# Moving the deviation and the normalisation of the gated values inside the feature stage of a one-core decoder step

## The reference, cut to what matters

```python
def gmlp_gate(u, v, ws, bs, ln_g, ln_b):
    u = jax.nn.gelu(u)
    vn = layer_norm(jax.nn.gelu(v).reshape(b, t, G_B, DG_B), ln_g, ln_b)
    ...
    mixed = jnp.einsum('gts,bnsgd->bntgd', w, vn.reshape(b, nc, c, G_B, DG_B))
    mixed = mixed + jnp.swapaxes(bs[:, :c], 0, 1)[:, :, None].astype(vn.dtype)
    return u * mixed.reshape(b, t, W_B), vn.reshape(b, t, W_B)
```

## Time and profile before

| | |
|---|---|
| median of 3 runs | 1611.86 us (1606.54 to 1611.88) |
| the profiled execution, its time | 1607.65 us |
| its span in the trace | 1605.9 us |
| TensorE busy | 1392.5 us, 87% of the span |
| VectorE, ScalarE, GpSimd busy | 644.2, 549.5, 158.1 us |
| mean granted TensorE clock | 0.928 of full speed |
| feature stage, TensorE's last product to next stage's first | 12.14 us without a matmul |

### The profile page before, as it was taken

How to read it: one execution, slowest core, us unless ns; L and a number is a source line. 1 busy time by engine, 2 the same in 40 slices (tenths; PEclk the granted TensorE clock), 3 DMA queues, 4 the chain that set the end, 5 groups by cost and what they waited for, 6 DMA issues and landing times. The chain is left out here.

```text
span 1605.9 us, 25617 instructions
## 1 busy us (share of the span) xinstructions
PE 1392.5 (87%) x9998; PEld 982.1 (61%) x9999; DVE 644.2 (40%) x1021; ACT 549.5 (34%) x1070; POOL 158.1 (10%) x152
## 2 busy tenths in 40 slices
PE   4998999689999989887997998989982799998980
PEld 2444999665568767776886996767862233333320
DVE  3331554248731223343875002337546223322226
ACT  1222324148740633444222213433120343332325
POOL 0000000003310023220000000000000122222210
PEclk9999999879997979999998999999995799999995
DMA  9111121114001340001304104635234488787336
GB/s 329 51 49 40 33 59 40 50 54 157 1 27 34 100 145 16 2 3 37 131 40 144 40 14 171 249 106 175 106 127 187 175 275 284 245 303 237 83 62 226
DMA packets 83684, 185.03 MB, mean 115 GB/s; under 512 B 12948, under 2 KB 48923, under 8 KB 77171
## 3 DMA queue, kind: packets, MB, share of 16 engines
q1 hardware_dynamic: 76523, 157.14, 27.6%
q0 software_dynamic: 6912, 25.17, 6.7%
q10 hardware_dynamic: 144, 1.25, 0.2%
HBM read 144.31 MB, written 39.31 MB: 114 GB/s over the span
## 5 line engine op out<-in xcount | busy, mean ns | idle before, releaser
L3068 PE MATMUL bank<-arena,hT 128*64 x384 | 178.0, 608 | 10.1 <-DVE hT L3184 5.7
L3068 PEld LDWEIGHTS bank<-arena,hT 128*64 128x64 f32 x384 | 51.4, 140 | 112.4 <-issue 109.6
L479 PE MATMUL bank<-arena,hT 128*128 128x512 f32 x256 | 112.1, 596 | 0.0
L2140 PE MATMUL bank<-hT_rest,f_w_high 128*128 128x352 f32 x288 | 93.9, 326 | 0.0
L3071 PE MATMUL bank<-arena,hT 128*64 128x512 f32 x192 | 91.0, 620 | 0.0
L3094 PE MATMUL bank<-arena,hT 128*64 x192 | 87.5, 598 | 0.7 <-ACT hT L3135 0.7
L3071 PE MATMUL bank<-h,hT 128*64 128x512 f32 x192 | 87.0, 596 | 0.0
L479 PEld LDWEIGHTS bank<-arena,hT 128*128 128x128 f32 x256 | 48.5, 192 | 57.9 <-issue 57.9
L3024 POOL DMA_INDIRECT expert_sums<-hT,row_slot x24 | 47.4, 1973 | 222.0 <-DVE hT L3190 142.4
L2139 PE MATMUL bank<-hT_high,q_w_high 128*128 128x352 f32 x192 | 62.5, 326 | 4.0 <-DVE q_w_low L2432 4.0
L2139 PE MATMUL bank<-f_h_high_a,f_w_high 128*128 128x352 f32 x180 | 59.2, 329 | 6.7 <-DVE f_w_low L689 6.7
(11 more groups left out here) (494 smaller groups left out, 3181.2 us busy)
## 6 DMA issues: line engine op xcount, KB each, us to landing
arena<-in_ex_wg_dram SPq DMA_DIRECT2D x16, 1024.0 KB, 4.9
arena<-in_ex_wu_dram SPq DMA_DIRECT2D x16, 1024.0 KB, 8.5
arena<-in_ex_wd_dram SPq DMA_DIRECT2D x16, 1024.0 KB, 12.3
tokens<-h SPq DMA_DIRECT2D x24, 512.0 KB, 2.6
arena<-in_cache_mem_k_dram SPq DMA_DIRECT2D x8, 1024.0 KB, 4.9
arena<-in_w_in_dram SPq DMA_DIRECT2D x12, 512.0 KB, 4.0
h<-tokens SPq DMA_DIRECT2D x6, 1024.0 KB, 7.2
h<-in_x_prompt_dram SPq DMA_DIRECT2D x8, 512.0 KB, 8.7
```

The lines of the kernel that those rows point to most:

```text
L479: last = nc.tensor.matmul(ps[bank][0:r, 0:n], hT[:, k, i * P:i * P + r], wt[:, k, col:col + n], start=(k == 0), stop=(k == KC - 1))
L2140: nc.tensor.matmul(out, high, w_low, start=False, stop=False)
L3068: nc.tensor.matmul(ps[UPB[u % 2]][rows_of(0), :], xT[:, u % 2, k, rows_of(0)], gate_up_of[:, bass.ds(slot, 1), :, k, :].rearrange("p a g f ...
```

## The change

ScalarE's table load, its wait for `stats` and its two instructions for the deviation stand in the loop over blocks behind block 2. On VectorE the wait for the deviation and the three passes stand between `low_w(10)` and `low_w(11)`.

```diff
                 if n == 2:
                     act.wait_ge(cw_mm, 1)
                     nc.scalar.copy(cw, ps[7][:, 0:168].rearrange("p (c n) -> p c n", c=6)).then_inc(cw_ok, 1)
+                if n == 2:
+                    nc.scalar.preload_act_table_set(EXPLN)
+                    act.wait_ge(stats, 1)
+                    link(nc.scalar.activation(mom[:, 1, :], mom[:, 1, :], ACT.Ln, bias=c.eps, scale=1.0 / DH))
+                    nc.scalar.activation(mom[:, 1, :], mom[:, 1, :], ACT.Exp, scale=-0.5).then_inc(rstd_ok, 1)
                 if n >= 4:
                     if n - 4 < 6:
                         conv_silu(n - 4)
-            nc.scalar.preload_act_table_set(EXPLN)
-            act.wait_ge(stats, 1)
-            link(nc.scalar.activation(mom[:, 1, :], mom[:, 1, :], ACT.Ln, bias=c.eps, scale=1.0 / DH))
-            nc.scalar.activation(mom[:, 1, :], mom[:, 1, :], ACT.Exp, scale=-0.5).then_inc(rstd_ok, 1)
...
-            for n in range(10, len(plan)):
-                low_w(n)
+            low_w(10)
             dve.wait_ge(rstd_ok, 1)
             link(nc.vector.tensor_tensor(vg, vg, bc(mom[:, 1, :]), ALU.mult))
             dve.wait_ge(ln_in, 32)
             link(nc.vector.tensor_tensor(c.vg, c.vg, c.A("glng").unsqueeze(1).to_broadcast([P, TILES, 256]), ALU.mult))
             nc.vector.tensor_tensor(c.vg, c.vg, c.A("glnb").unsqueeze(1).to_broadcast([P, TILES, 256]),
                                     ALU.add).then_inc(normed, 1)
+            low_w(11)
```

## The result

The changed kernel takes 1600.15 us, the median of 6 runs (1594.65 to 1602.94), against 1610.69 us for the kernel before (6 runs, the three of the table above among them): a ratio of 0.9933, 95% interval 0.9911 to 0.9956. It is faster: the medians lie 10.5 us apart, and the ratio stands for 10.8. Two later comparisons, on other sets of runs, gave 1600.32 against 1607.54 (0.9942, 0.9920 to 0.9964) and 1595.40 against 1608.13 (0.9933, 0.9912 to 0.9955), so the medians lay 7.2 and 12.7 us apart there. One run of all those in this document, with two idle passes (see the experiments), took 2426.97 us at a mean granted clock of 0.553 and is left out of its median. The profiled execution took 1600.09 us, its span is 1598.3 us, 7.6 us under before's.

What follows compares the result with a forecast made beforehand. TensorE was taken as the bound, so only its standstill at the feature stage's end could pay. 11.3 + 1.0 = 12.3 us off 1611.86 gave 1599.6 us; the range was reasoned from 1592.9 up to 1605.

Steps and rivals of the forecast that it cites:

- The tail: Feature stage's end, after ScalarE's last evacuation: 11.60 us to the next stage's first issue, so the stage should end 11.3 us earlier.
- Part one, ScalarE behind block 2: Moved work of about 1.9 us fits 4.48 us free there; cost 0, bounds 0 and 1.9 us lost.
- the rule on grouping by set: Objection to ScalarE's new place: one added table switch at 2.66 us would make the gain 8.6 us instead of 11.3.
- Part two, VectorE between the roundings: Between `low_w(10)` and `low_w(11)`: three passes need 7.7 of 11.27 us free; cost 0, adding nothing to part one.
- the edge at 289.9 us: Latest end of VectorE's passes ahead of `low_w(11)` before TensorE waits at block 11: 291.12 less 1.22.
- What is late next: TensorE's last group and evacuation at 303.32, then the gate stage's pooling-table load holding the first diffs, 6.3 us.
- The clock in the gate stage: Low clock costs 2.3 us there before; a later fall gains 1.0 us, bounds 2.3 gained and 1.8 lost.
- The rival by the rule: Gate stage: a 1 us boundary alone doesn't throttle, the clock stays high, 2.3 us gained, 1598.3 us; chance 0.20.
- It moves with the stage's start, and so does everything after.: The pooling-table load and all later work shift with the gate stage's earlier start; no earlier-issued transfer must still land.
- The slower rivals: Gate stage's clock stays at 1.2 GHz: 1613.0 us, chance 0.04; VectorE's passes end late, starving block 11: 1615, chance 0.02.

Runs made afterwards that it cites:

- two idle passes: Changed kernel with two idle VectorE passes added behind the last evacuation, meant to start later stages 2.5 us later; 1599.41 us, ratio to before 0.9935.
- the late passes: Kernel before with ScalarE's deviation moved early, but VectorE's three passes waiting for the last evacuation; 1607.17 us, ratio to before 0.9999.
- the early deviation alone: Kernel before with only ScalarE's part of the change, VectorE's passes staying behind the last rest (`low_w(11)`); 1601.78 us, ratio to before 0.9949.
- three passes more: Changed kernel with three extra VectorE passes, leaving the values as they are, ahead of the last rest (`low_w(11)`); 1599.47 us, ratio to before 0.9941.
- five: Changed kernel with five extra VectorE passes, leaving the values as they are, ahead of the last rest (`low_w(11)`); 1602.27 us, ratio to before 0.9964.
- the kernel with the tables early: Changed kernel with the pooling tables loaded under block 11 instead of at the gate stage's head; 1594.68 us, then 1593.70 us.

## Why the prediction was right

**The forecast** was 1599.6 us in a range of 1592.5 to 1605.0; 1600.15 was measured. The mechanism was right: 12.3 us were forecast for the feature and the gate stage together, and they came out 11.4 + 0.7 = 12.1 us shorter in the trace. That the median came within 0.6 us is luck. The median of before moved from 1611.86 to 1610.69 with three more runs, the measured gain was 10.5 us, and the same two kernels lay 7.2 and 12.7 us apart in the later sets, where the changed one had 1600.32 and 1595.40.

**The tail** (11.60 us less 0.29 for the meeting): 11.60 - 0.27 = 11.33 in the trace after. Its parts are confirmed by the late passes (9.66 us without ScalarE's share) and the whole by the early deviation alone (feature stage 147.9 us).

**Part one, ScalarE behind block 2:** taken at 0, and 0. Nothing behind it came late and no table load was added. On the rule on grouping by set, from the Trainium skill, "ScalarE: Activation LUTs", section "Table sets: the hidden batching unit": it spoke of a cost per switch, and here the number of switches stayed. The load that was moved took 1.28 us, and the logarithm started 1.30 us after the load did, so the page's 2.66 us for a switch is not what this trace has.

**Part two, VectorE between the roundings:** taken at 0, and 0; that it adds nothing to part one held, and so did the edge at 289.9 us: three passes more ended there without a wait, and the wait with five puts it at 289.7.

**What is late next:** TensorE's last group and its evacuation, then the tables, as said; loading them early took TensorE's wait away.

**The clock in the gate stage:** taken as a fall that comes later, worth 1.0 us, between 2.3 gained and 1.8 lost. It fell at about 306; the two tiles that the earlier trace rows show slow took 3.31 + 2.15 us in place of 3.92 + 2.71, so 1.2 us were gained there, and the stage is 0.7 us shorter. Most of the difference was lost at its end, for which the forecast had no term: the clock fell before the stage's last product (L835), which took 1.03 us where L834 had taken 0.60. The rival by the rule from "TensorE: Matmul & The Clock Gate" in the Trainium skill, section "What's actually happening", that the boundary alone doesn't throttle, was right about the boundary: the clock was at 2.4 GHz until 306. In the light work behind it, it fell all the same, except in one trace of the kernel with the tables early, where it stayed up until 325.

**The step that was short:** "It moves with the stage's start, and so does everything after." The transfers do, and no later stage has a new wait (behind the gate stage TensorE waits for 121.6 us in all after the change, 122.4 before). But I gave the clock a term in the gate stage alone. Against the first trace of before, the sample attention gained 2.4 us and the delta stage lost 6.0 us, with more of the stage at the high clock in the one (mean 0.81 against 0.79) and less in the other (0.90 against 0.94). Both lengths also vary between traces of the changed kernel alone (63.4, 65.7 and 62.5 us; 193.0, 193.0 and 187.2 us), so they can't be put down to the change as such. They are half its size, and with 1.0 us lost in the rest they are why the profiled spans are only 7.6 us apart. That last 1.0 us is open: the stage behind the delta stage took 214.3 us in all three traces of the changed kernel and 213.5 and 213.3 in the two of before. I had put the places in which the runs lie down to scatter; for the changed kernel the traces show a stage 250 us behind the change as the larger part of it.

The slower rivals didn't come: TensorE had its clock back at 313, in the second tile, and VectorE's passes kept their 2.56 us beside TensorE.

## What to carry to other kernels

When all engines meet at a stage's end, read what runs between the last product and the meeting: work whose inputs were ready long before belongs under the matmuls, and moving the first, smallest link of the chain (here two activations of 0.3 and 0.2 us) can be what frees the whole of it. Price the cover by the consumer's start less the producer's own time, and test it on both sides of that edge. And before a difference of a few us between two traces is explained by a change, cut both into stages: here an untouched stage differed by 5.8 us between executions of one program.

## What was not expected of the hardware

The granted clock fell to 1.2 GHz while TensorE was busy for over 90% of the time, as this profile counts it: in the changed kernel's delta stage it was busy for 9.44 of the 10 us ahead of the fall at the full clock, and for 9.39 and 9.48 of 10 in the windows behind it. In the third trace of the same kernel it was busy for 9.26 of 10 us, the clock stayed up there, and the stage was 5.8 us shorter. The Trainium skill, "TensorE: Matmul & The Clock Gate", section "What's actually happening", says that the length of a slow start varies from run to run of one kernel. These runs show a variation of that kind in mid-kernel, in the gate stage with the tables early (26.0 and 24.7 us) and in the delta stage; whether it has the page's cause, no run here shows. The traced runs of the changed kernel lie in two places, 6 to 8 us apart, of which the delta stage and the one in front of it make 4.6.
